# Two residual layers (RWKV-7 with a dense FFN, S5 with experts): the FFN's norm put on its gate and up sums, one PE block moved, the FFN's sums added bank by bank

## The reference, cut to what matters

```python
def rmsnorm(x, g):
    y = xf * rsqrt(mean(xf * xf, axis=-1, keepdims=True) + NORM_EPS)
    return y * g
for i in range(DEPTH):                      # DEPTH = 2
    hn = rmsnorm(h, norm_mix[i])
    mix = rwkv7_time_mix(hn, ...)           # layer 0; layer 1: s5_mixer(hn, ...)
    h = h + mix
    hn = rmsnorm(h, norm_ffn[i])
    ffn = (silu(hn @ w_gate) * (hn @ w_up)) @ w_down    # layer 1: moe_swiglu
    h = h + ffn
return rmsnorm(h, final_norm)
# in rwkv7_time_mix, per head of 64 channels:
kk = kk / maximum(norm(kk, axis=-1), 1e-12)             # the keys' norm
```

## Time and profile before

| | us |
|---|---|
| median of 3 runs | 1642.6 |
| the profiled execution, its own time | 1643.39 |
| its span in the trace | 1641.5 |
| PE busy in the span | 1576.6 (96%) |
| DVE busy | 1270.2 (77%) |
| ACT busy | 958.2 (58%) |
| mean granted TensorE clock (1 is full) | 0.979 |

### The profile page before, as it was taken

The page is one execution under the profiler, slowest core; times in us unless marked ns, Lnnn a source line. Parts: engine busy times, 40 slices in busy tenths (PEclk is TensorE's granted clock), DMA queues, the critical chain, the costliest instruction groups (busy, mean ns, idle before and its releaser), DMA issues.

```text
span 1641.5 us, 28526 instructions
## 1 busy us (share of the span) xinstructions
PE 1576.6 (96%) x12396; PEld 1359.9 (83%) x12396; DVE 1270.2 (77%) x1430; ACT 958.2 (58%) x1054; POOL 87.8 (5%) x71
## 2 busy tenths in 40 slices
PE   8898798899998999999999999999999999999997
PEld 7698787899998788788888888888888888888885
DVE  6675432996865546998988888888888898988985
ACT  2723211666441036776776776776776777777673
POOL 0006101100001600000000000000000000000000
PEclk9999999999996999999999999999999999999999
DMA  7230002444525064799799799799799799799791
GB/s 287 94 130 28 4 3 104 153 182 164 184 90 207 20 265 187 290 384 372 295 392 384 284 392 399 272 389 401 268 392 402 269 390 401 276 384 401 276 382 68
DMA packets 72493, 421.19 MB, mean 257 GB/s; under 512 B 5024, under 2 KB 5152, under 8 KB 37424
## 3 DMA queue, kind: packets, MB, share of 16 engines
q1 hardware_dynamic: 72016, 418.26, 65.5%
q0 software_dynamic: 352, 1.10, 0.2%
HBM read 418.29 MB, written 1.05 MB: 255 GB/s over the span
## 4 chain that ended last, share of the span: by engine, by line
PE 91%; DVE 4%; POOL 2%; issue 1%; ACT 1%; DVEq 0%; POOLq 0%
PE PS L1285 37%; PE PS L1298 18%; PE PS L1100 11%; PE PS L1208 3%; PE PS L1314 2%; PE PS L733 2%; PE PS L1085 2%; PE PS L710 2%; PE PS L1291 1%; PE PS L887 1%; PE PS L754 1%; PE PS L692 1%; PE PS L904 1%; DVE LOA L1791 1%; PE PS L1174 1%
## 5 line engine op out<-in xcount | busy, mean ns | idle before, releaser
L1791 DVE TENSOR_TENSOR LOA<-EXA,WH 128x2048 fp32r<-128x2048 f32 x224 | 504.7, 2289 | 94.1 <-ACT WH L598 94.1
L598 ACT ACTIVATE WH<-EXA 128x2048 fp32r<-128x2048 f32 x224 | 416.9, 1909 | 6.4 <-DMA EXA<-in_wmoe 6.2
L1285 PE MATMUL PS<-WH,XGH 128*128 128x512 f32 x896 | 360.6, 403 | 0.0
L1285 PE MATMUL PS<-WH,XGL 128*128 128x512 f32 x896 | 350.6, 391 | 0.0
L1285 PE MATMUL PS<-LOA,XGH 128*128 128x512 f32 x896 | 350.0, 391 | 0.0
L1797 DVE TENSOR_TENSOR LOB<-EXB,WH 128x1024 fp32r<-128x1024 f32 x224 | 264.3, 1222 | 8.6 <-ACT WH L602 8.5
L602 ACT ACTIVATE WH<-EXB 128x1024 fp32r<-128x1024 f32 x224 | 224.2, 1052 | 0.0
L1285 PEld LDWEIGHTS PS<-WH,XGL 128*128 128x128 f32 x896 | 168.2, 188 | 35.7
L1285 PEld LDWEIGHTS PS<-WH,XGH 128*128 128x128 f32 x896 | 168.4, 188 | 33.4 <-DVE XGL L1889 1.8
L1285 PEld LDWEIGHTS PS<-LOA,XGH 128*128 128x128 f32 x896 | 168.8, 188 | 31.2
L1298 PE MATMUL PS<-WH,MHH 128*128 128x512 f32 x448 | 174.6, 390 | 3.8 <-DVE MHL L1885 3.8
(11 more groups left out here) (413 smaller groups left out, 2410.9 us busy)
## 6 DMA issues: line engine op xcount, KB each, us to landing
EXA<-in_wmoe SPq DMA_DIRECT2D x112, 2048.0 KB, 8.6
EXB<-in_wmoe SPq DMA_DIRECT2D x112, 1024.0 KB, 8.1
FRA<-in_wffn SPq DMA_DIRECT2D x22, 1024.0 KB, 5.9
RING<-in_wsq SPq DMA_DIRECT2D x16, 1024.0 KB, 4.9
FRB<-in_wffn SPq DMA_DIRECT2D x22, 512.0 KB, 3.8
GLUW<-in_wglu SPq DMA_DIRECT2D x8, 1024.0 KB, 12.5
LORA<-in_lora SPq DMA_DIRECT2D x1, 1536.0 KB, 18.4
CON<-in_con SPq DMA_DIRECT2D x1, 1156.0 KB, 20.6
```

What stands on the lines that cost most here:

```text
L598: act.activation(WH[:, n % 4, 0:NARROW], EXA[PAIR_SLOT[n // 2]][:, n % 2, :], ACT.Copy).then_inc(S("m_ahi"), 1)
L1285: mm = pe.matmul(PS[:, p % 2, :], x[:, k, :], w, start=k == 0 and m == 0, stop=k == KC - 1 and m == 2)
L1791: tt(LOA[slot][:, n % 2, :], EXA[slot][:, n % 2, :], WH[:, n % 4, 0:NARROW].bitcast(F32), ALU.subtract)\
```

## The change

There are three edits.

1. **The token's factor is moved behind the gate and up products.** `FH` and `FL` are now made from `HT` times the channel gain only, chunk by chunk, as soon as a pair of chunks of `HT` is complete. The factor `NT` is applied in each FFN step by one new DVE instruction on the gate and up sums (128x512). The silu then reads that result, and no longer PSUM. The first weights are loaded and split earlier, `WHI`/`WLO` use the other of two buffers, and the last `norm_part` stands between the gate half and the up half of step 0.
2. **PE's `spread` of the keys' norm** stands behind `project_split(2)` and no longer ahead of it.
3. **The FFN's sums are added to `HT` by bank** (4 pieces, each as soon as its bank is complete), with the squares and `norm_part` in 4 pieces too.

```diff
 # ACT
 for t in range(4):
     act.wait_ge(S("h_out"), t + 1)
+    for j in (2 * t, 2 * t + 1):
+        act.activation(FH[:, j, :], HT[:, j, :], ACT.Copy, scale=prm("ffn0", j)).then_inc(S("f_hi"), 1)
     square(1, SQB, slice(2 * t, 2 * t + 2))
+    if t == 1:
+        ffn_hi_a(0, 0); ffn_hi_a(0, 1)
 act.wait_ge(S("used"), 16)
-ffn_hi_a(0, 0)
+ffn_hi_a(1, 0)
 root(1)
-ffn_hi_a(0, 1)
-ffn_hi_a(1, 0)
-for n in range(4): ... FH from HNF
 ffn_hi_a(1, 1)
 ffn_hi_b(0)
...
 for t in range(NFFN):
-    act.wait_ge(S("f_ps"), t + 1)
-    act.activation(FSG[:, t % 2, :], half(t % 3, 0), ACT.Silu).then_inc(S("f_silu"), 1)
+    act.wait_ge(S("f_mul"), 2 * t + 1)
+    act.activation(FGU[:, t % 2, 0, :], FGU[:, t % 2, 0, :], ACT.Silu).then_inc(S("f_silu"), 1)
     round_back(t, 0)
     if t + 2 < NFFN:
         ffn_hi_a(t + 2, 0)
-    act.wait_ge(S("f_mul"), t + 1)
+    act.wait_ge(S("f_mul"), 2 * t + 2)
...
 # PE
 project_split(1, XRH, XRL)
+project_split(2, XRH, XRL)
 ...spread...
-project_split(2, XRH, XRL)
 project_split(3, XRH, XRL)
...
     for h in range(2):
         if t == 0 and h == 1:
+            norm_part(1, SQB, 3, False, True, 2)
             pe.wait_ge(S("f_alo"), 2)
...
 ffn_down(NFFN - 1)
-pe.wait_ge(S("h_out"), 6)
-norm(2, SQB)
+for g in range(NG):
+    norm_part(2, SQ2, g, g == 0, g == NG - 1, 2)
 # DVE
 for t in range(4): ... HT += a bank of the mixer's output
+    if t == 2:
+        ffn_lo_a(0, 0); ffn_lo_a(0, 1)
+    for j in (2 * t, 2 * t + 1):
+        stt(FL[:, j, :], HT[:, j, :], prm("ffn0", j), FH[:, j, :].bitcast(F32), ALU.mult, ALU.subtract).then_inc(S("f_lo"), 1)
-norm(1, "ffn0", HNF[:, :, :], lambda: ffn_lo_a(0, 0), input_low)
+... variance; ffn_lo_a(1, 0); reciprocal of the root, kept in NT
...
 for t in range(NFFN):
-    dve.wait_ge(S("f_silu"), t + 1)
-    tt(FHF[:, t % 2, :], FSG[:, t % 2, :], half(t % 3, 1), ALU.mult).then_inc(S("f_mul"), 1)
+    dve.wait_ge(S("f_ps"), t + 1)
+    tt(FGU[:, t % 2, :, :], PS[:, t % 3, :]..., by_token, ALU.mult).then_inc(S("f_mul"), 1)
     if t + 2 < NFFN:
         ffn_lo_a(t + 2, 0)
+    dve.wait_ge(S("f_silu"), t + 1)
+    tt(FGU[:, t % 2, 1, :], FGU[:, t % 2, 0, :], FGU[:, t % 2, 1, :], ALU.mult).then_inc(S("f_mul"), 1)
     dve.wait_ge(S("f_hh"), t + 1)
     tt(FHL..., ALU.subtract).then_inc(S("f_hl"), 1)
     if t + 2 < NFFN:
         ffn_lo_a(t + 2, 1)
...
-for n, h in enumerate(halves): HT += PS banks 4+2n, 5+2n
+for g in range(NG): wait for bank 4+g, HT += it
```

More of the change, by code:

```diff
@@ L587, in _ @@
                 between(t)
-            for n, h in enumerate(halves):
-                act.wait_ge(S("h_out"), 5 + n)
-                square(2, SQB, h)
+            for g in range(NG):
+                act.wait_ge(S("h_out"), 5 + g)
+                square(2, SQ2, slice(2 * g, 2 * g + 2))
             root(2)
@@ L1118, in ffn_down @@
                 for n in range(KC):
-                    mm = three(half(4 + n // 2, n % 2), t % 2, NARROW + n * P, lambda k: FHH[:, t % 2, :],
+                    mm = three(half(4 + n // 2, n % 2), (t + 1) % 2, NARROW + n * P, lambda k: FHH[:, t % 2, :],
                                lambda k: FHL[:, t % 2, :], 1, t == 0 and n % 2 == 0, True)
+                    if t == NFFN - 1 and n in (1, 3, 5):
+                        mm.then_inc(S("f_ps"), 1)
                 mm.then_inc(S("used"), 1)
@@ L1168, in drive @@
                     if part == 0 or cc == 0:
[L1169 removed]
+                        pe.wait_ge(S("n_out"), 8 + (c + 1 if part == 0 else KC))
                     for m in range(2):
@@ L1599, in _, with ffn_lo_a, ffn_lo_b @@
                 tt(flat(T1[:, pair, :]), flat(YY[:, pair, :]), flat(T3[:, pair, :]), ALU.add).then_inc(S("yg"), 1)
+            def ffn_lo_a(t, h):
+                dve.wait_ge(S("f_ahi"), 2 * t + h + 1)
+                cols = slice(h * D, (h + 1) * D)
+                tt(WLO[:, (t + 1) % 2, cols], FRA[:, t % 2, cols], WHI[:, (t + 1) % 2, cols].bitcast(F32), ALU.subtract)\
+                    .then_inc(S("f_alo"), 1)
+            def ffn_lo_b(t):
+                dve.wait_ge(S("f_bhi"), t + 1)
+                tt(WLO[:, (t + 1) % 2, NARROW:WIDE], FRB[:, t % 2, :], WHI[:, (t + 1) % 2, NARROW:WIDE].bitcast(F32), ALU.subtract)\
+                    .then_inc(S("f_blo"), 1)
             for t in range(4):
@@ L1746, in _ @@
                 prepare(t)
[L1747 to L1750, removed]
+            for g in range(NG):
+                pair = slice(2 * g, 2 * g + 2)
+                if g < NG - 1:
+                    dve.wait_ge(S("f_ps"), NFFN + g + 1)
+                else:
+                    dve.wait_ge(S("used"), NSQ + NFFN)
+                tt(flat(HT[:, pair, :]), flat(HT[:, pair, :]), PS[:, 4 + g, :], ALU.add).then_inc(S("h_out"), 1)
+            dve.wait_ge(S("h_out"), 8)
             norm(2, "mix1", HN[:, :, :])
```

73 lines of the change are left out of this document (33 added, 40 removed).

## The result

| | us, median | runs |
|---|---|---|
| before | 1645.86 (1641.24 to 1648.58) | 6 |
| after | 1668.83 (1664.5 to 1673.35) | 6 |

A forecast was written before the change was run, and what follows sets the result against it. PE was taken to set the FFN's pace at 8.64 us a step, with DVE and ACT the bound after. -5.9 + 30.3 - 4.2 = +20.2 gave 1663.6, or 1662.8 us on the median; 8 in 10: 1653 to 1669.

The forecast's parts named there:

- the first edit's term: FFN, start included: DVE and ACT become the bound, PE's end moves from 496.5 to 526.8, +30.3 us.
- steps 9 and 10: FFN steps with little to prepare, where PE is the bound: 17.4 us for the two.
- steps 19 to 21: Last FFN steps, PE's again: 19.0 us, ending at 526.8.
- shifts as a whole: Everything behind `drive` waits only for what runs ahead of it, so it moves without a change of its own.
- The pace of the steps: DVE's FFN steps: 11.35 us with complex products, 10.65 with sine tables, both above PE's 8.64.
- The four additions: Added to DVE's FFN step: scaling 0.60, waiting for the first high part 1.5, unhidden `FHH` 0.55, second high part 0.6 us.
- PE's wait for `FHL`: FFN sign in the profile after: PE waits for `FHL` about 2 us a step.
- The second edit: Keys' norm: third R item ahead of the spread, -5.9 us, with a new 1.35 us wait; bounds -6.9 to -4.5.
- The third edit: FFN's end: last matmul to `drive` 6.85 us where it was 11.0, -4.2 us; -2.5 if the clock falls.
- The bound beside it: `drive` at the full clock: its 256 matmuls at about 0.029 instead of 0.051 each, up to 5.6 us more gained.
- The start of the first edit: FFN's start: gate_up(1) at 295.3 instead of 300.8 before the second edit's shift, -5.5 us, with a 3.9 us stretch carried over.
- the rival: Clock falls in PE's new FFN pauses: +1 to +8 us, 1664 to 1671; 8% for more than +4.

The follow-up runs named there:

- e8: Changed kernel with POOL's two memsets put behind DVE's six small S5 operations at the FFN's start: 1667.48 us, ratio 1.0153 to the kernel before.
- e3: Changed kernel with ACT's first high part of the next weights issued ahead of the silu that waits for DVE's scaling: 1642.82 us, ratio 0.9984 to before.
- e4: e3 plus the second high part ahead of `FHH` on ACT and the second low part ahead of `FHL` on DVE: 1639.69 us, ratio 0.9962 to before.
- e7: Changed kernel without the scaling product per token; silu and DVE's product read PSUM as before: 1631.5 us, ratio 0.9912 to before.
- e2: Kernel before with only the third edit (FFN sums, squares and norm parts by bank): 1642.04 us, ratio 0.9977 to before.
- e1: Changed kernel with only the second edit undone, the spread again ahead of the third R item: 1677.35 us, ratio 1.0195 to before.
- e6: e4 plus 24 matmuls whose sums nothing reads, in PE's pause ahead of `drive`: 1640.57 us, ratio 0.9966 to before.
- e5: e4 with all S5 parameter operations moved into DVE's pauses between the mixer's last additions, plus an unused root on ACT: 1627.03 us, ratio 0.9886 to before.

## Where the prediction was right, and where it failed

**The step that failed: the size of the first edit's term, "+30.3 us", with bounds of 27.5 to 33.** By the traces it is +36.5: the FFN's last matmul ends 30.5 us later, although the stretch ahead of the FFN had become 6.0 shorter. The mechanism behind the term came as forecast; two of its parts were too small. One is the start, where a stretch was carried over as it was (1.9 us). The other is the steps in which PE is the bound, 17.4 for steps 9 and 10 and 19.0 for steps 19 to 21: they were priced at the full clock and took 19.2 and 20.9 (17.7 and 19.4 in e8, where the clock stayed up in them). Besides, the line "shifts as a whole" put the difference behind `drive` at nothing, and in this execution it was 2.3.

**The pace of the steps: right.** Forecast 11.35 us with complex products and 10.65 with sine tables; measured 11.37 and 10.77. Steps 1 to 8 were to last 93.6 us and lasted 93.61. The four additions are visible one by one: 1.43, 0.48 and 0.52 us of idling in the rows above, and the scaling's start-to-start of 0.60. They add up to 3.03 of the 3.25 by which the step grew; the rest is start overlap, since behind a pause an instruction doesn't begin before the one ahead has ended. e3, e4 and e7 take the additions away in turn, and the step follows: 9.84, 8.72, 8.12. PE's wait for `FHL`, forecast at about 2 us a step, shows in eight steps only, 13.0 us in all. The silu takes 0.42 us from SBUF, 0.39 before from PSUM, as the forecast's rows had it.

**The second edit: right.** Forecast -5.9 with a new wait of 1.35 us. The chain of waits of the changed kernel, 60 to 130 us:

```profile
78.13 1.08 PE PS L791 x16
79.21 5.94 PE PS L733 x48
85.14 1.37 issue
86.51 11.74 PE PS L733 x96
98.25 3.46 PE PS L779 x16
```

The spread runs at the full clock (1.08 us, 2.09 before by the earlier trace rows) and the new wait is 1.37. The sums begin 6.4 earlier, of which 0.8 was there before the first K item ended: -5.6. A slip in the working did no harm: 78.9 and 1.05 give 79.95 for the spread's end, not 80.15; the wait for `RLO` takes up the difference.

**The third edit: right.** Forecast 6.85 from the last matmul to `drive`, measured 6.9 in the changed kernel and in e2. The bound beside it, up to 5.6 us for a faster `drive`, was read too small: it counts 256 matmuls, and `drive` has 512. The gain did not come: the clock fell in `drive` here too.

**The start of the first edit: too small.** gate_up(1) was to begin at 289.4 and began at 291.35, and DVE's step 1 at 305.66 in place of 303.8. What failed is the line "from the end of the last of these to gate_up(1) it was 3.9 us before": it carried a stretch over as it was, but the earlier start laid it beside POOL's memset, and it took 5.3. In e8, with the memset later, it takes 3.9 again, and gate_up(1) comes 1.4 us sooner. (Of the pauses at the start the reading named only the larger: the view of the earlier trace rows also has 0.6 us at `norm_part`, for the squares.)

**The clock: the rival came in small.** It had 8% for more than 4 us. In the profiled execution of the changed kernel the granted clock fell seven times in the FFN, at 289.1, 323.3, 340.3, 384.7, 401.8, 490.5 and 511.0 us, each time during a pause of PE or within 1.6 us behind one. Five of the falls cost no time that the steps show. One of them, in step 2, with busy time and granted clock:

```profile
323.00:327.00 4.00, 4.00 (x23) 4.00 (x22) 3.93 (x6) 2.47 (x5) 0.00 (x0) 0.57 0.37 82
```

That step takes 11.38 us, and 11.37 in e8, where the clock is 1.00 in it. As the rival's "against" had it, a fall doesn't count where DVE is the bound. The other two lie where PE is the bound. The first, in step 9:

```profile
400.00:401.00 1.00, 0.00 (x0) 0.00 (x0) 0.00 (x0) 1.00 (x3) 0.00 (x0) 1.00 0.65 270
...
402.00:403.00 1.00, 1.00 (x7) 1.00 (x7) 1.00 (x1) 0.00 (x0) 0.00 (x0) 0.50 0.00 0
```

and the second, where the sines are done, in PE's last 120 matmuls of the FFN, in the chain of waits:

```profile
510.81 16.16 PE PS L1099 x120
```

120 matmuls at 0.12 us are 14.4; they took 1.8 more. Step 9 took 9.67 us and step 20 6.27. In e8, whose code is the same there, they took 8.27 and 4.77, and its clock was 1.00 in both places, though PE paused there for 1.9 us as well:

```profile
399.30:415.00 15.70, 15.70 (x132) 15.70 (x133) 9.70 (x13) 12.30 (x19) 0.00 (x0) 1.00 0.29 101
507.50:522.00 14.50, 14.45 (x120) 14.48 (x121) 9.75 (x16) 6.93 (x11) 0.00 (x0) 1.00 0.00 1
```

So those two falls are worth about 2.9 us of the profiled execution. They are no accident of it alone: e1, whose FFN is the same code, has all seven falls at the same places of the FFN, 6.1 us later. In e8 it fell six times, three of them at the same places, the others elsewhere. What decides where a fall comes stays open.

**Behind `drive`: not the plain shift that was forecast.** From the start of `drive` to the end the changed execution has 1136.4 us and the one before 1134.0. The work there is the same in all ten traces, and they make two groups: 1134.0 to 1134.8 before and in e2, e4, e6, e7 and e8, 1136.2 to 1136.4 in the changed kernel, e1, e3 and e5. e4, e6, e7 and e8 have all that the changed kernel has behind `drive`, so this 2.3 us is a difference between executions; its cause was not traced.

The sum of the misses in the trace: 1.9 at the start, 1.8 in steps 9 and 10, 0.5 in steps 11 to 18, 1.9 in steps 19 to 21, 2.3 behind `drive`: 8.4, against 1672.1 - 1663.6 = 8.5. On the medians it is 6.0, and in e8, without the first term at gate_up(1) and without the two falls that count, the FFN took 244.2 us where the forecast had 242.0. That the medians come nearer to the forecast than the profiled execution is no merit of the working: that execution is 3.2 us above the median of its kernel.

## What to carry to other kernels

When an operation is put between two engines that each work through their queue in order, look first at what now stands behind the new wait: a transfer or a conversion that is ready long before should be issued ahead of the instruction that waits for the other engine. Here that order cost some 30 us (33 with the two falls of the clock in it) and the operation itself 5, and the order is repaired by moving three lines. Small operations that wait for each other belong into a pause of the engine that is full later, and a stretch that is moved in time has to be laid beside the other engines anew.

## What the runs showed of the hardware

- A `TENSOR_SCALAR` of 128x32 out of SBUF takes 0.17 us, and took 2.60 in the changed kernel, e1, e3, e4, e6 and e7, ending within 0.1 us of POOL's memset; in e8 one of 0.98 us did so. A `TENSOR_TENSOR` with both inputs in SBUF, `WLO`, took its usual 1.22 us while the same memset ran (283.66 in the changed kernel), and so did the reciprocal with 1.75 and a `TENSOR_SCALAR` out of PSUM with 0.42 (283.32). The Trainium skill ("SBUF — State Buffer", Who interferes with whom) has both halves: a tensor_scalar may take the ports that DVE shares with GpSimd and then one blocks the other for the whole instruction, while an operation with two SBUF inputs meets only GpSimd's reads. The traces agree with both.
- The 3.44 us pause ahead of `drive` is not needed for the low clock in it: with matmuls right up to its start, the granted clock was 1.00 for its first 5.5 us and 0.50 from the gap of 1.33 us on that follows. It then stayed 0.50 to the end of `drive`, with PE busy all the time (8.00 of 8.00 us from 512 to 520), and so it does in the nine other traces, where it falls between 1.0 us ahead of `drive`'s first matmul and 1.8 us behind it.
- Pauses of 1.9 us of PE were followed by clock 0.50 in some places and not in others: in the changed kernel behind those that end at 384.6, 401.0, 489.3 and 510.8 us, but not behind the one at 478.5; in e8 behind those at 382.9 and 475.2, but not at 399.3, 496.8 and 507.6.
